# Mixture-of-experts stage of a one-layer diffusion backbone: 128-row expert passes, and a token sort by matrix product

## The reference, cut to what matters

```python
def _moe(h, router_w, router_b, w_gate, w_up, w_down):
    ...
    g = jnp.argmax(gscore, axis=-1)                  # one group of 4 experts per token
    ...
    _, loc = lax.top_k(in_group, TOP_K)              # two experts in that group
    expert = g[:, None] * EXPERTS_PER_GROUP + loc
    ...
    hg = jnp.einsum('td,edf->tef', h, w_gate)        # 1024 -> 512
    hu = jnp.einsum('td,edf->tef', h, w_up)          # 1024 -> 512
    act = jax.nn.silu(hg) * hu * gates[..., None].astype(h.dtype)
    return jnp.einsum('tef,efd->td', act, w_down)    # 512 -> 1024
```

## Time and profile before

| | us |
|---|---|
| median of 3 runs (616.27 to 617.57) | 616.38 |
| the profiled execution | 621.26 |
| its span, first to last instruction | 619.4 |
| mean granted clock of TensorE | 0.908 |
| busy: TensorE / weight load / VectorE / ScalarE / GpSimd | 492.6 / 234.0 / 224.1 / 142.8 / 86.1 |
| DMA | 164.52 MB, mean 266 GB/s |

### The profile page before, as it was taken

How to read it: one execution, slowest core, us unless ns; L and a number is a source line. 1 busy time by engine, 2 the same in 40 slices (tenths; PEclk the granted TensorE clock), 3 DMA queues, 4 the chain that set the end, 5 groups by cost and what they waited for, 6 DMA issues and landing times.

```text
span 619.4 us, 7520 instructions
## 1 busy us (share of the span) xinstructions
PE 492.6 (80%) x2624; PEld 234.0 (38%) x2625; DVE 224.1 (36%) x616; ACT 142.8 (23%) x263; POOL 86.1 (14%) x177
## 2 busy tenths in 40 slices
PE   1769889999989999950479899999988878788800
PEld 1225688544478544630243233333332222222200
DVE  3589855999982105560020010110110010101027
ACT  3555842601148201300030010110110010100023
POOL 2000603888000151013000000000000000000030
PEclk9998989999989999975589999999998797978965
DMA  8980340733994931049648993879999999996162
GB/s 296 366 329 0 120 136 6 286 136 120 388 387 183 378 147 43 26 159 392 263 168 335 391 379 108 353 301 411 431 424 423 423 423 422 423 423 266 35 215 107
DMA packets 38032, 164.52 MB, mean 266 GB/s; under 512 B 2776, under 2 KB 3544, under 8 KB 32240
## 3 DMA queue, kind: packets, MB, share of 16 engines
q1 hardware_dynamic: 31120, 145.79, 59.9%
q10 hardware_dynamic: 4608, 10.86, 4.8%
q0 software_dynamic: 2272, 7.46, 3.4%
HBM read 152.76 MB, written 11.34 MB: 265 GB/s over the span
## 4 chain that ended last, share of the span: by engine, by line
issue 51%; PE 30%; DVE 7%; DMA 5%; ACT 4%; POOL 1%; ACTq 0%; POOLq 0%; DVEq 0%
PE psum L604 7%; PE psum L487 3%; PE psum L553 3%; PE psum L479 3%; DMA arena<-in_x_sample 3%; PE psum L509 3%; PE psum L578 3%; PE psum L418 2%; DMA arena<-in_w_mod 2%; PE psum L598 2%; PE psum L628 1%; ACT arena L802 1%; POOL sorted_tokens L1519 1%; DMA arena<-sorted_outputs,pos_u 1%; PE psum L496 1%
## 5 line engine op out<-in xcount | busy, mean ns | idle before, releaser
L676 PE MATMUL psum<-arena 128*64 128x512 f32 x672 | 165.2, 648 | 31.5 <-DMA arena<-in_w_up 21.2
L676 PEld LDWEIGHTS psum<-arena 128*64 128x64 f32 x672 | 51.9, 148 | 131.2 <-issue 111.6
L689 PE MATMUL psum<-arena 128*64 128x512 f32 x336 | 75.8, 592 | 2.3 <-ACTq L972 2.3
L1364 DVE TENSOR_TENSOR arena<-arena,psum 128x256 f32<-128x256 f32 x21 | 8.9, 422 | 183.4 <-ACT arena L956 183.4
L1527 POOL DMA_INDIRECT arena<-sorted_outputs,pos_u x6 | 5.7, 952 | 308.6 <-DMA sorted_outputs<-arena 307.1
L689 PEld LDWEIGHTS psum<-arena 128*64 128x64 f32 x336 | 25.1, 137 | 48.8 <-issue 48.8
L956 ACT ACTIVATE arena<-psum 128x256 f32<-128x256 f32 x21 | 8.1, 384 | 146.2 <-PE psum L676 130.7
L604 PE MATMUL psum<-arena 128*128 128x512 f32 x96 | 41.5, 592 | 0.0
L418 PE MATMUL psum<-arena 128*2 128x256 f32 x256 | 30.7, 395 | 0.3 <-DMA arena<-in_w_mod 0.3
L660 PE MATMUL psum<-arena 128*128 128x128 f32 x48 | 6.7, 302 | 27.0 <-DMA arena<-sorted_tokens 27.0
L961 ACT ACTIVATE arena<-psum 128x512 f32<-128x512 f32 x21 | 12.5, 597 | 66.7 <-PE psum L689 66.7
(11 more groups left out here) (278 smaller groups left out, 586.2 us busy)
## 6 DMA issues: line engine op xcount, KB each, us to landing
arena<-in_w_gate SPq DMA_DIRECT2D x16, 2048.0 KB, 17.5
arena<-in_w_up SPq DMA_DIRECT2D x16, 2048.0 KB, 22.3
arena<-in_w_down SPq DMA_DIRECT2D x16, 2048.0 KB, 19.8
arena<-in_w_mod SPq DMA_DIRECT2D x12, 2048.0 KB, 13.8
arena<-in_w_in SPq DMA_DIRECT2D x3, 2048.0 KB, 19.1
sorted_outputs<-arena ACTq DMA_DIRECT2D x42, 128.0 KB, 6.5
arena<-in_w_out SPq DMA_DIRECT2D x2, 2048.0 KB, 17.5
arena<-modulation_rows ACTq DMA_DIRECT2D x3, 1024.0 KB, 11.2
```

What stands on the lines that cost most here:

```text
L676: last = mm(bank[0][HALF * t:HALF * t + HALF, :], xs[:, k, :], gu[:, :, k, t * 256:t * 256 + 256], start=(k == 0), stop=(k == KD - 1))
L689: last = mm(bank[4][HALF * h:HALF * h + HALF, :], hiddenT[:, s * P + t * HALF:s * P + t * HALF + HALF], dn[:, 2 * t + s, h * 512:h * 512 + ...
```

## The change: what it does

- A pass is 128 rows wide if an expert has more than 64 (`gate_up_wide`, `down_wide`: the same number of products, one after the other, with 128 rows as the stationary operand; the hidden values are 128x512, and gate and up have a bank each). An expert with up to 64 rows is worked on as before (`gate_up_narrow`, `down_narrow`). An expert with more than 128 rows gets its rest in `extra_pass`, one or two of 128 rows, in which gate/up, silu, product, transposes and down follow one another.
- `PASSES` is 3. The release of a buffer set is counted in steps of two per expert; for a wide expert the second step of `gated` comes where its own pass is through (and, above 128 rows, after its extra passes).
- The token sort: VectorE makes matrices that have a one where a token's place equals the column's number (`places` for the places 0 to 511, `far_places` for 512 to 767). TensorE multiplies the transposed tokens with them, summed over the three tiles of 128 tokens. The results are sorted and transposed, and are copied to `hTs`. The indirect writes, `sorted_tokens` and its loads are gone. The far places are done after the first expert's gate/up.
- Set 2 of the weight buffers moves: gate and up to where the output projection's weights were, so its first load waits only for that projection (`wo_ready`); down to where `h2` is.

```diff
-SORTED = PAIRS + 2 * P
+SORTED = PAIRS + P
 SETS = 3
-PASSES = 6
...
-        hsr = view(slot(7), 6, D)
+        NEAR = 512
+        places = view(F + 10240, NT, NEAR)
+        far_places = view(F + 12288, NT, PAIRS - NEAR)
+        numbers = view(F + 13056, PAIRS)
+        numbers_i = view(F + 10240, PAIRS).bitcast(I32)
         hTs = view(F + 3072, KD, SORTED)
-        xs = view(F + 11264, KD, HALF)
-        hiddenT = view(F + 11776, 256)
-        sg = view(F + 12032, 256)
-        hidden = view(F + 12288, 256)
-        ystage = view(F + 12544, 3, 512)
+        xs = view(F + 10240, KD, P)
+        hidden = view(F + 11264, 512)
+        hiddenT = view(F + 11776, 512)
+        ystage = view(F + 12288, 2, D)
...
-            b = (3, 0, 6)[j]
-            return view(slot(b), 2, KD, DE), view(slot(b + 2), 4, D)
+            gu, dn = ((3, 5), (0, 2), (7, 6))[j]
+            return view(slot(gu), 2, KD, DE), view(slot(dn), 4, D)
...
-                sp.wait_ge(S("gated"), (e - 2) * PASSES)
+                sp.wait_ge(S("gated"), 2 * (e - 2))
                 load_gate_up(j, e)
-                sp.wait_ge(S("downed"), (e - 2) * PASSES + 1)
+                sp.wait_ge(S("downed"), 2 * (e - 2))
                 load_down(j, e)
 
...
+            sp.wait_ge(S("wo_ready"), 6)
+            load_gate_up(2, 2)
             sp.wait_ge(S("unit_used"), 15)
             load_gate_up(1, 1)
             sp.wait_ge(S("yt_done"), 4)
             sp.wait_ge(S("modd_in5"), 16)
             load_down(1, 1)
-            for t in range(6):
-                if t == 0:
-                    sp.wait_ge(S("tok_sent"), 16 * 6)
-                sp.dma_start(hsr[:, t, :], hsd[t * P:(t + 1) * P, :]).then_inc(S(f"hs_in{t}"), 16)
-            sp.wait_ge(S("hs_ready"), 12)
-            sp.wait_ge(S("pad_sent"), 32)
-            load_gate_up(2, 2)
+            sp.wait_ge(S("sort_ready"), 12)
+            sp.wait_ge(S("sort_copied_v"), 6)
+            sp.wait_ge(S("pad_sent"), 16)
             load_down(2, 2)
...
+            def tokens(t, k):
+                return h2[:, t, :].rearrange("p (q k) -> p k q", k=KD)[:, k, :]
...
+            for t in range(NT):
+                pe.wait_ge(S("places_made"), t + 1)
+                for k in range(KD):
+                    last = mm(bank[k][:, :], tokens(t, k), places[:, t, :], start=(t == 0), stop=(t == NT - 1))
+                    if t == NT - 1:
+                        last.then_inc(S("sort_ready"), 1)
...
+            def gate_up_wide(j, sem):
 
                 gu = expert_weights(j)[0]
-                pe.wait_ge(S("x_staged"), at + 1)
-                if fresh is not None:
-                    pe.wait_ge(S(f"gu_in{j}"), fresh * 32)
+                for k in range(KD):
+                    for h in range(2):
+                        last = mm(bank[h][:, :], xs[:, k, :], gu[:, h, k, :], start=(k == 0), stop=(k == KD - 1))
+                last.then_inc(S(sem), 1)
...
+                last.then_inc(S("gated"), 2)
...
+            def down_wide(j, sem, inc):
+                for c in range(4):
+                    for h in range(2):
+                        last = mm(bank[4 + h][:, :], hiddenT[:, c * P:c * P + P], dn[:, c, h * 512:h * 512 + 512],
+                                  start=(c == 0), stop=(c == 3))
+                last.then_inc(S(sem), inc)
...
-                last.then_inc(S("downed"), 1)
...
+                last.then_inc(S("downed"), 2)
+
+            def transposes(n, sem):
+
+                for c in range(n):
+                    last = tr(bank[2][:, c * P:c * P + P], hidden[:, c * P:c * P + P], ident[:, :])
+                last.then_inc(S(sem), 1)
...
+            def first_pass(j, e, fresh, between):
+
+                pe.wait_ge(S("x_staged"), e + 1)
+                pe.wait_ge(S(f"gu_in{j}"), fresh * 32)
                 n = pe.value_load(n_i[0:1, bass.ds(e, 1)], min_val=0, max_val=NT * P)
                 with pe.If(n > HALF):
-                    gate_up(j, turn(1, e), None)
-                    down(j, use + 1, turn(1, e), turn(0, e))
-                    transposes(turn(1, e))
-                    with pe.If(n > P):
-                        gate_up(j, turn(2, e), None)
-                        down(j, use + 1, turn(2, e), turn(1, e))
-                        transposes(turn(2, e))
-                        with pe.If(n > P + HALF):
-                            with pe.Fori(3, PASSES) as q:
-                                gate_up(j, q + turn(0, e), None)
-                                down(j, use + 1, q + turn(0, e), q + turn(0, e) + -1)
-                                transposes(q + turn(0, e))
-                        with pe.Else():
-                            skipped(e, 3)
+                    gate_up_wide(j, "gated")
+                    between()
+                    pe.wait_ge(S("multiplied"), e + 1)
+                    transposes(4, "crossed")
+                with pe.Else():
+                    gate_up_narrow(j)
+                    between()
+                    pe.wait_ge(S("multiplied"), e + 1)
+                    transposes(2, "crossed")
+
+            def extra_pass(j, e, q):
+
+                pe.wait_ge(S("extra_vector"), extra(e, q, 1, 3))
+                gate_up_wide(j, "extra_product")
+                pe.wait_ge(S("extra_vector"), extra(e, q, 2, 3))
+                transposes(4, "extra_product")
+                pe.wait_ge(S("extra_vector"), extra(e, q, 3, 3))
+                if q == 0:
+                    pe.wait_ge(S("evacuated"), e + 2)
+                else:
+                    pe.wait_ge(S("extra_scalar"), extra(e, 0, 2, 2))
+                down_wide(j, "extra_product", 1)
...
+            def expert(j, e, use):
+
+                nothing = lambda: None
+                m = pe.value_load(n_i[0:1, bass.ds(e, 1)], min_val=0, max_val=NT * P)
+                following = ((j + 1) % SETS, e + 1, use + (j + 1) // SETS + 1)
+                with pe.If(m > HALF):
+                    with pe.If(m > P):
+                        down(j, e, use + 1, True, 1)
+                        extra_passes(j, e, m)
+                        pe.wait_ge(S("extra_product"), extra(e, 2, 0, 3))
+                        pe.sem_inc(S("gated"), 1)
+                        pe.sem_inc(S("downed"), 1)
+                        pe.wait_ge(S("extra_scalar"), extra(e, 2, 0, 2))
+                        first_pass(*following, nothing)
                     with pe.Else():
-                        skipped(e, 2)
+                        pe.sem_inc(S("gated"), 1)
+                        pe.sem_inc(S("extra_product"), 6)
+                        first_pass(*following, lambda: down(j, e, use + 1, True, 2))
                 with pe.Else():
-                    skipped(e, 1)
-
-            pe.sem_inc(S("downed"), 1)
-            gate_up(0, 0, 1)
-            for t in range(1, 6):
-                sorted_columns(t)
+                    pe.sem_inc(S("extra_product"), 6)
+                    first_pass(*following, lambda: down(j, e, use + 1, False, 2))
...
+            def other_columns():
+                pe.wait_ge(S("far_places_made"), NT)
+                for k in range(KD):
+                    for t in range(NT):
+                        last = mm(bank[(3, 6, 7, 4)[k // 2]][:, (k % 2) * 256:(k % 2) * 256 + 256], tokens(t, k),
+                                  far_places[:, t, :], start=(t == 0), stop=(t == NT - 1))
+                    if k % 2 == 1:
+                        last.then_inc(S("sort_ready"), 1)
+
+            first_pass(0, 0, 1, other_columns)
...
+                    with act.If(m > P):
+                        evacuate_wide(e, y)
+                        extra_passes(e, y, m)
+                        act.wait_ge(S("written"), all_written(e, 3))
+                        gate(e + 1)
                     with act.Else():
-                        skipped(e, 2)
+                        gate(e + 1)
+                        evacuate_wide(e, y)
+                        no_extra()
                 with act.Else():
...
+            dve.wait_ge(S("numbers_made"), 1)
+
+            def place(out, c, sem):
+                for t in range(NT):
+                    first, second = g1.rearrange(flat)[:, t:t + 1], g1.rearrange(flat)[:, NT + t:NT + t + 1]
+                    v(ts(out[:, t, :], numbers[:, c], first, None, ALU.is_equal))
+                    stt(out[:, t, :], numbers[:, c], second, out[:, t, :], ALU.is_equal, ALU.add).then_inc(S(sem), 1)
+
+            place(places, slice(0, NEAR), "places_made")
+            place(far_places, slice(NEAR, PAIRS), "far_places_made")
+
...
+            def stage_x(row, sem):
+
+                cp(xs[:, :, :], hTs[:, :, bass.ds(row, P)]).then_inc(S(sem), 1)
...
+            def extra_pass(e, q):
+
+                row = dve.value_load(off_i[0:1, bass.ds(e, 1)], min_val=0, max_val=PAIRS - P * (q + 1))
+                stage_x(row + P * (q + 1), "extra_vector")
+                dve.wait_ge(S("extra_scalar"), extra(e, q, 1, 2))
```

(26 more changed lines are left out.)

310 lines of the change are left out of this document (149 added, 161 removed).

## The result

| | before | changed |
|---|---|---|
| median, us | 616.33 | 724.03 |
| ratio (95% interval) | | 1.174 (1.169 to 1.179) |
| profiled execution / its span, us | 621.26 / 619.4 | 725.03 / 723.2 |
| routing done to the end of the last down, us | 312.8 | 423.5 |
| instruction packets in the execution | 19 | 66 |

Slower was forecast, but 641 (628 to 653). The fourth line of the table goes from VectorE's cast to `pos_u` (275.77 before, 268.92 after) to the end of the last down (588.56 and 692.39). It takes out what stands ahead of the routing, where nothing was changed and where these two executions differ by 6.9 us. It grew by 110.7 us.

A forecast was written before the change was run, and what follows sets the result against it. The end was taken to be set by when the weight stream becomes continuous, at the fourth expert's last down. 621.26 + 24.7 - 0.4 = 645.6 profiled, median 4.9 below: 640.7, said as 641, range 628 to 653.

The forecast's parts named there:

- the second branch and the jumps: TensorE's first five experts: 0.3 to 2 us each, taken at 0.7, so -2 to +6 us on the sum.
- it is DMA that sets it there again: Tenth expert on: TensorE's own path (488.9) is within 491.0, so weight loads set the pace, experts 15.5 us apart.
- code loading: Rival: jumps in TensorE's first five experts cost 1 to 2 us each, 6 to 15 more, 647 to 656; chance 0.12.
- The stream of weights: Seventh expert's down load waits for the fourth's last down, at 440.6 against 415.94; the stream ends 24.7 us later.
- The wide pass: TensorE's 128-row passes: gate/up 13.8 us, down 6.9, exactly twice the narrow ones.
- The sort: Token sort on TensorE: 20.7 us plus 2.6 for the clock, first gate/up at 303.3 against 303.91; far places 10.3.
- The third expert: Its wide pass and extra pass on TensorE put the fourth expert's gate/up at 406.5, 23.7 us later.
- The clock: TensorE slow after pauses: 0 to 3 us at five places, 10.1 taken in all, so -8 to +4.
- No more gaps than before: Rival: 10.6 us of gaps again up to the fourth expert's last down, 13.3 later, 629 us; chance 0.14.
- faster: Rival: the weight stream is not held and, with 4 MiB less, ends 10.3 us sooner, 606 us; chance 0.04.
- does nothing: Rival: no expert has more than 64 rows, so only the sort differs, 617 to 621 us; chance 0.03.
- likeliest case: The forecast itself, summed over the whole kernel: 641 us, reaching from 634 to 649; chance 0.67.

The follow-up runs named there:

- a_compact: The changed kernel with TensorE's branches laid out one behind the other in place of one copy for each combination, same work; 655.24 us, ratio 1.062.
- b_pad24: The kernel before with 24 never-run products added in each expert's branch for over 192 rows; 637.49 us, ratio 1.031.
- b_sort: The kernel before with the new token sort and the early gate/up load of set 2, keeping its 64-row passes; 619.98 us, ratio 1.003.
- a_hybrid: a_compact with an extra pass of 64 rows in place of 128 for the third expert; 642.83 us, ratio 1.040.

## Why the prediction was wrong, point by point

**The step that failed** is the term for "the second branch and the jumps", taken at 0.7 us with a bound of 0.3 to 2 us in each of the first five experts, and with it the sentence that from the tenth expert on "it is DMA that sets it there again". The mechanism stood among the rivals, as code loading, at 6 to 15 us more and a chance of 0.12. Its size was 69 us (724 to 655, by a_compact), with some 6 more that a_compact still pays in its first turn, and it didn't end with the fifth expert: from the eighth on an expert took 20.2 us in the mean, so TensorE, not the stream, set the end. The one row that I had for it was a stall of 1.19 us, and I multiplied it by the number of jumps. What it could not tell is that before the loop was kept from its second turn on: 19 packets of instructions in the whole execution, of which 1 after 420 us, and that one after 575, at the end of the last turn. That line, with a count of the loop's products, 312 and 630, was there to be read before. It would have asked the question that no row answered: how much is kept? The Trainium skill has the rule (Runtime: NRT & Kernel Launch, Instruction fetch mechanics: a taken branch out of the loaded window of two pages waits for a fetch). The runs agree that such a fetch is waited for, but not on the window: its pages are of 256 instructions, and the loop of 312 products, 1248 instructions at four a product, turned without a packet from 420 to 575 us. By the profile's counts a product is four instructions (672 matmuls and 672 weight loads in 336 products). The same section of the Trainium skill gives TensorE room for 2048 instructions; b_pad24's loop, 1536 of these and its register, branch and semaphore instructions, which were not counted, already stalls. The measurement decides.

**The stream of weights.** Right where TensorE's code is kept. In a_compact the fourth expert's last down ends 176.4 us after the cast (140.1 before), 36.3 later, and the sixteenth's gate/up starts 321.3 after it (283.5 before), 37.8 later. The predicted shift was 24.7. Of the 11.6 more, 6.2 are the gap ahead of the second expert (8.3 where I had 2.1). The gaps ahead of the fourth and fifth, without fetches, are 4.0 and 2.8 where I had 3.4 and 2.1, 1.3 together. The clock was slower than I took at three places: 16.4 for the fourth's gate/up (15.3), 8.8 for the fifth's (7.1) and 8.8 for the extra pass' down (6.9), 4.7 together. The other terms take 0.6 off.

**The wide pass.** Right: 13.90 us for 32 matmuls at full clock (I had 13.8), 7.1 for the down (6.9), and nothing given back for two narrow ones. The Trainium skill's "Always tile to 128 partitions" (Trainium Kernel Development and Optimization, Best Practices), read as a rule of speed, would have been wrong here: two narrow gate/ups take 2 x 7.09 = 14.2 us and a wide one 13.9.

**The sort.** Right in its two halves: 23.9 us (I had 23.3) and a first gate/up 28.0 us after the cast (27.5); far places 11.6 (10.3). Alone, the sort and the early load are worth 1.003 (b_sort), and the early 4 MiB nothing, as said.

**The third expert.** The gaps were 1.41 ahead of the transposes and 0.86 ahead of the down (I had 1.8 and 1.1). The extra pass' width cost 12.4 to 13.7 us (a_hybrid; I had 11).

**The clock.** Wide gate/ups behind a pause took 15.69 to 16.55 (13.9 otherwise), so 1.8 to 2.7 in place of my 1.5.

**The rivals.** "No more gaps than before" (629) and "faster" (606) were wrong, and so was "does nothing". With the code kept, the likeliest case's own terms give 641 to a measured 655, still 14 short: about 6 are the fetches in the first turn, and about 5 the clock after pauses.

What stays open: the exact amount of code that is kept, in bytes and packets, and whether its alignment matters. Which engine the packets of queue 8 belong to isn't recorded; that the pads were in TensorE's code alone, and that its branch is what came late, is the ground for putting them there. No version beat the kernel before.

## What to carry to other kernels

Before you add variants of a body to a loop, count the engine's instructions in one turn, run or not, and look at the packets of the instruction queue in the loop's later turns: if there are none, the loop is kept, and that is something that can be lost. Put alternatives one behind the other (gate/up either way, then down either way), not one copy of the whole for each combination: here that alone was 69 us. And two 64-row products side by side are as fast as one of 128 rows, so a wider pass gains nothing by itself and costs a full one for the last few rows.

## What the runs showed of the hardware that was not expected

- TensorE's code was kept up to 354 to 360 fp32 products in a loop (7 packets after 330 us) and fetched again from 384 on (34 packets).
- Gaps from fetches go in steps of about 2.2 us with idle DMA engines and of about 4.4 beside a stream of weights, where three packets make 12.3 us.
- VectorE's copy of 1024 columns in on-chip memory takes 0.69 us where 512 took 0.43, so staging twice the rows costs 0.27 more.
